# First projection of a decoder layer: waiting for the transposed activations block by block

## The chip, the cores and the metric

The kernel runs on one core of a Trainium2 chip. The metric is device time in microseconds (us), the median of several executions; lower is better.

## The reference

One layer of a decoder over 512 positions of width 2048, in float32:

```
h    = rmsnorm(x, attn_norm)
proj = einsum('bsd,de->bse', h, w_in)        # q, k, v of group A; q, k, v of group B
out_a = dilated_attention(...)               # 16 heads, three dilated windows, ALiBi
out_b = swa_sink_attention(...)              # 16 heads on 2 kv heads, window 128, sinks
x = x + concat(rmsnorm(out_a), rmsnorm(out_b)) @ w_out
x = x + (silu(h2 @ w_gate) * (h2 @ w_up)) @ w_down,   h2 = rmsnorm(x, ffn_norm)
return rmsnorm(x, final_norm)
```

What matters here is the very beginning: loading x, transposing it, and the first two projections (k and v of group B, 128 columns each).

## The kernel before

Each float32 operand of a large product is kept as two halves that TensorE takes, a rounded one (`_hi`) and the remainder (`_lo`), and a product is three matmuls: hi·hi, hi·lo, lo·hi (`three`, lines 285 to 287). ScalarE (ACT) makes the hi half with an activation, VectorE (DVE) the lo half from it.

**Weights** come in units of 512x128, one DMA of 256 KB each, into one of four slots of `raw`. `split` turns a slot into `w_hi` (ACT, L601) and `w_lo` (DVE, L878); a reload of a slot waits for `w_lo`. A unit (u4, slot) serves four blocks of 128 rows of the contraction. Four units make one projection. In what follows unit 0 to 3 is the first projection (bank Q), unit 4 to 7 the second (bank K).

**x** comes in eight DMAs of 512 KB (`x_loaded[0..7]`), each with two blocks k of 128 columns. The SP queue issues ident, then x pieces 0, 1, weight (0,0), x 2, 3, weight (0,1), x 4, 5, weight (0,2), x 6, 7, weight (0,3), then the weights of units 4 to 7. For each block k of the 16, `turn_x` does four TensorE transposes into one of four PSUM banks (L295), `x_high` makes `h_hi` on ACT with the gain of the norm (L606), `x_low` makes `h_lo` on DVE (L882), and signals `xt_lo_done`, which frees the bank for block k+4. The gains themselves arrive as rows, are transposed on TensorE (L488) and copied by DVE (L1062, `gains_done`); every `x_high` needs them.

**Order on TensorE (PE):** blocks 0 to 7 are transposed first (with the gains after block 1). Unit 0 then waits for its four blocks at once, unit 0's twelve matmuls follow, then transposes 8 to 11, unit 1, transposes 12 to 15, unit 2, unit 3. Units 4 to 7 follow, with one thing before unit 7: `spread_r` (L302), eight instructions that spread 1/rms over a bank and wait for `wide_done`. After that the attention pairs begin.

**Order on ACT:** x_high 0-3; w_hi of (0,0) and (0,1); x_high 4-7; w_hi (0,2); four squares of x (L614); x_high 8-11; w_hi (0,3), (1,0); x_high 12-15; w_hi (1,1); four squares; eight small DMA issues; w_hi (1,2); four squares. The last of these squares lets DVE form the row means, GpSimd (POOL) the power, and DVE `widen_r` (L908, `wide_done`).

**Order on DVE:** four memsets, the copy of the gains, x_low 0-3, w_lo (0,0), (0,1), and so on in the order of ACT. Both queues are written out by hand, and every instruction waits its turn.

Of the kernel before, what the change touches and what calls it, by code (L numbers as in the profile page):

```python
# [6 lines left out]
ACT = mybir.ActivationFunctionType  # L7
# [5 lines left out]
P = 128  # L13
# [10 lines left out]
KD = D // P  # L24
# [18 lines left out]
BANK_Q, BANK_K, BANK_V = 0, 1, 4  # L43
# [3 lines left out]
BANK_X = (2, 3, 5, 7)  # L47
BANK_GATE, BANK_UP = (2, 5), (3, 7)

START_SPLITS = ([(0, 0), (0, 1)], [(0, 2)], [(0, 3), (1, 0)], [(1, 1)])  # L50
FIRST_SQ = 4 * (NC - 1)

LAST = [(t, n) for n in range(NC) for t in (0, 1)] + [(t, n) for t in (2, 3) for n in range(NC)]
# [16 lines left out]
def build(nc, x, attn_norm, w_in, sinks, out_norm_a, out_norm_b, w_out, ffn_norm,  # L70
# [4 lines left out]
    def sb(name, shape, dt=F32, at=None):  # L75

        place = spot[0] if at is None else at
        size = int(np.prod(shape[1:])) * BYTES
        t = nc.alloc_sbuf_tensor_at(name, shape, dt, offset=place)
        if at is None:  # L80
            spot[0] = place + (size + 31) // 32 * 32
        assert place + size <= nc.sbuf_usable_end, name
        ends[name] = place + size
        return t

    ends = {}
    ident = sb("ident", [P, P])
    ones = sb("ones", [P, P])
# [5 lines left out]
    tick = sb("tick", [P, 20])  # L94
# [5 lines left out]
    w_hi = sb("w_hi", [P, RING, UNIT], F32R)  # L100
    w_lo = sb("w_lo", [P, RING, UNIT], F32R)
    place_x = spot[0]
    h_hi = sb("h_hi", [P, KD, SEQ], F32R)
    place_y = spot[0]
    h_lo = sb("h_lo", [P, KD, SEQ], F32R)
# [7 lines left out]
    x_first = sb("x_first", [P, NT, D], at=place_o)  # L113
# [41 lines left out]
    bank = [nc.alloc_psum_tensor(f"bank{i}", [P, 512], F32) for i in range(8)]  # L155

    def sem(name):
        return nc.alloc_semaphore(name)

    raw_loaded = [sem(f"raw_loaded{i}") for i in range(RING)]  # L160
    w_hi_done, w_lo_done, w_used = sem("w_hi_done"), sem("w_lo_done"), sem("w_used")
    x_loaded = [sem(f"x_loaded{i}") for i in range(2 * NC)]
    x_again = [sem(f"x_again{i}") for i in range(NC)]
    consts_loaded, ident_loaded, ones_done, gains_loaded = sem("consts_loaded"), sem("ident_loaded"), sem("ones_done"), sem("gains_loaded")
    xt_ready, xt_hi_done, xt_lo_done = sem("xt_ready"), sem("xt_hi_done"), sem("xt_lo_done")
    sq_done, sq_last_done, total_done, mean_done, inv_done = sem("sq_done"), sem("sq_last_done"), sem("total_done"), sem("mean_done"), sem("inv_done")
    wide_done, rbc_ready, rbc_done = sem("wide_done"), sem("rbc_ready"), sem("rbc_done")
    acc_taken, gains_turned, gains_done = sem("acc_taken"), sem("gains_turned"), sem("gains_done")
# [22 lines left out]
    gain_rows = probs[0]  # L191
# [13 lines left out]
    def x_bank(k, base):  # L205

        return bank[(BANK_G if base and k >= KD - 4 else BANK_X)[k % 4]]
# [74 lines left out]
    def _(pe):  # L282
        def three(out_ap, st_hi, st_lo, mv_hi, mv_lo, start, stop):

            nc.tensor.matmul(out_ap, st_hi, mv_hi, start=start, stop=False, skip_group_check=True)  # L285
            nc.tensor.matmul(out_ap, st_hi, mv_lo, start=False, stop=False, skip_group_check=True)  # L286
            return nc.tensor.matmul(out_ap, st_lo, mv_hi, start=False, stop=stop, skip_group_check=True)  # L287

        def turn_x(src, k, base):

            if base + k >= 4:
                pe.wait_ge(xt_lo_done, base + k - 3)
            b = x_bank(k, base)
            for t in range(NT):
                mm = nc.tensor.transpose(b[:, P * t:P * (t + 1)], src[:, t, P * k:P * (k + 1)], ident[:, :])  # L295
            mm.then_inc(xt_ready, 1)

        def spread_r(wide, count, b):

            pe.wait_ge(wide_done, count)  # L300
            for t in range(NT):
                mm = nc.tensor.matmul(bank[b][:, P * t:P * (t + 1)], wide[:, t, :], ident[:, :], start=True, stop=True)  # L302
            mm.then_inc(rbc_ready, 1)

        def tall_unit(u4, j, b, hh, hl):

            pe.wait_ge(w_lo_done, 4 * u4 + j + 1)
            for k in range(4):
                ws = slice(P * k, P * (k + 1))
                mm = three(bank[b][:, :], w_hi[:, j, ws], w_lo[:, j, ws], hh[:, 4 * j + k, :], hl[:, 4 * j + k, :],  # L310
                           j == 0 and k == 0, j == 3 and k == 3)
            mm.then_inc(w_used, 1)
# [143 lines left out]
        def pair(p, a, kv):  # L456

            for c, b in enumerate((BANK_Q, BANK_K, BANK_V, BANK_K)):
# [7 lines left out]
                for j in range(4):  # L466
# [6 lines left out]
                    if a is None and c == 3 and j == 2:  # L473
# [2 lines left out]
                        n = KD + 2 * PAIRS  # L476
                        nc.tensor.transpose(bank[BANK_PT][:, 0:n], gain_rows[0:n, P:2 * P], ident[0:n, 0:n]).then_inc(gains_turned, 1)

        pe.wait_ge(ident_loaded, 16)

        for k in range(8):
            if k % 2 == 0:
                pe.wait_ge(x_loaded[k // 2], 16)
            turn_x(x_first, k, 0)
            if k == 1:

                pe.wait_ge(gains_loaded, 16)
                nc.tensor.transpose(bank[BANK_Q][:, 0:KD], gain_rows[0:KD, 0:P],  # L488
                                    ident[0:KD, 0:KD]).then_inc(gains_turned, 1)
        pe.wait_ge(gains_done, 1)  # L490
        for s in range(8):
            if s < 4:
                pe.wait_ge(xt_lo_done, 4 * s + 4)
            tall_unit(s // 4, s % 4, (BANK_Q, BANK_K)[s // 4], h_hi, h_lo)
            if s < 2:
                for k in range(8 + 4 * s, 12 + 4 * s):
                    if k % 2 == 0:
                        pe.wait_ge(x_loaded[k // 2], 16)
                    turn_x(x_first, k, 0)
            if s == 6:  # L500
                pe.wait_ge(xt_lo_done, KD)
                spread_r(squares[:, :].rearrange("p (t c) -> p t c", c=P), 1, BANK_PT)
# [10 lines left out]
        for g in range(4):  # L513
            for s in range(16):
# [3 lines left out]
                if g == 1 and s == 2:  # L518
# [3 lines left out]
                    for i, kind in enumerate("AB"):  # L522
                        for t in range(NT):
                            mm = nc.tensor.matmul(bank[BANK_PT][:, 4 * i + t:4 * i + t + 1],
                                                  sq_sum[kind][:, P * t:P * (t + 1)], ones[:, 0:1], start=True, stop=True)
# [69 lines left out]
    def _(act):  # L595
        def split(u4, s, wait_slot=True):

            act.wait_ge(raw_loaded[s], 16 * (u4 + 1))
            if wait_slot:
                act.wait_ge(w_used, 4 * u4 + s - 3)  # L600
            nc.scalar.activation(w_hi[:, s, :], raw[:, s, :], ACT.Copy).then_inc(w_hi_done, 1)  # L601

        def x_high(hi, k, base, g0):

            act.wait_ge(xt_ready, base + k + 1)
            nc.scalar.activation(hi[:, k, :], x_bank(k, base)[:, :], ACT.Copy,  # L606
                                 scale=gains[:, g0 + k:g0 + k + 1]).then_inc(xt_hi_done, 1)
# [42 lines left out]
        def pt_high(a, h, r):  # L650
            kind, _, r0 = HEAD[h]
            n = P * sum(len(q) for _, q, _ in (PT_A if kind == "A" else PT_B)[r])
            act.wait_ge(pt_ready, ROUNDS * a + r0 + r + 1)
            if not (isinstance(a, int) and a == 0 and r0 + r < 2):
                act.wait_ge(pv_done, ROUNDS * a + r0 + r - 1)
            nc.scalar.activation(pt_hi[:, (r0 + r) % 2, 0:n], bank[BANK_PT][:, 0:n], ACT.Copy).then_inc(pt_hi_done, 1)  # L656
# [93 lines left out]

        act.dma_start(gain_rows[0:KD, 0:P], attn_norm[0, :].rearrange("(k p) -> k p", p=P)).then_inc(gains_loaded, 16)

        act.wait_ge(gains_done, 1)
        for n in range(NC):
            for k in range(4 * n, 4 * n + 4):
                x_high(h_hi, k, 0, G_ATTN)
            for u4, slot in START_SPLITS[n]:
                split(u4, slot, wait_slot=u4 > 0)
# [115 lines left out]
    def _(dve):  # L874
        def split(u4, s):

            dve.wait_ge(w_hi_done, 4 * u4 + s + 1)
            nc.vector.tensor_tensor(w_lo[:, s, :], raw[:, s, :], w_hi[:, s, :].bitcast(F32), ALU.subtract).then_inc(w_lo_done, 1)  # L878

        def x_low(hi, lo, k, base, g0):  # L880
            dve.wait_ge(xt_hi_done, base + k + 1)
            nc.vector.scalar_tensor_tensor(lo[:, k, :], x_bank(k, base)[:, :], gains[:, g0 + k:g0 + k + 1],  # L882
                                           hi[:, k, :].bitcast(F32), ALU.mult, ALU.subtract).then_inc(xt_lo_done, 1)
# [68 lines left out]
        def pt_low(a, h, r):  # L952
            kind, _, r0 = HEAD[h]
            n = P * sum(len(q) for _, q, _ in (PT_A if kind == "A" else PT_B)[r])
            buf = (r0 + r) % 2
            low_half(pt_lo[:, buf, 0:n], bank[BANK_PT][:, 0:n], pt_hi[:, buf, 0:n], pt_hi_done, ROUNDS * a + r0 + r + 1, pt_lo_done)
# [100 lines left out]
        for kind in "AB":  # L1057
            for h in range(2):
                rest = slice(DH * (1 - h), DH * (2 - h))
                nc.vector.memset(k_lo[kind][h][rest, :].bitcast(F32), 0.0).then_inc(k_rest_zero, 1)  # L1060
        dve.wait_ge(gains_turned, 1)
        nc.vector.tensor_copy(gains[:, 0:KD], bank[BANK_Q][:, 0:KD]).then_inc(gains_done, 1)  # L1062
        dve.wait_ge(gains_done, 1)
        for n in range(NC):
            for k in range(4 * n, 4 * n + 4):
                x_low(h_hi, h_lo, k, 0, G_ATTN)
            for u4, slot in START_SPLITS[n]:
                split(u4, slot)
# [277 lines left out]
```

## Time and profile before

| | |
|---|---|
| median of 3 runs | 2136.72 us (2136.47 to 2137.04) |
| the profiled execution, its own time | 2136.36 us |
| its span | 2134.6 us |
| PE busy | 2115.2 us, 99% |
| DVE busy, ACT busy | 1029.3 us (48%), 743.7 us (35%) |

The span is what the profile covers; 1.76 us of the profiled execution's own time lie around it. PE is busy nearly all of the span, so what matters is where it is not.

### The profile page before, as it was taken

How to read it: one execution, taken by the hardware profiler on the slowest of the kernel's cores; microseconds unless marked ns; L12 is line 12 of the kernel's file. 1: busy time of each engine (PE TensorE's matmuls, PEld its weight loads, DVE VectorE, ACT ScalarE, POOL GpSimd, SP SyncE). 2: the span in 40 equal slices, each digit the busy share in tenths (PEclk: the TensorE clock that was granted, in tenths of full speed). 3: DMA queues.
4: the chain of work that ended last, by engine and by line, in shares of the span. 5: the costliest groups of instructions: out<-in, count | busy, mean ns of one | idle time of the engine just before them, and what ended most of it. 6: DMA issues, size and time to landing. Idle time of an engine off the chain costs nothing.

```text
span 2134.6 us, 29372 instructions
## 1 busy us (share of the span) xinstructions
PE 2115.2 (99%) x9718; PEld 1754.6 (82%) x9718; DVE 1029.3 (48%) x1944; ACT 743.7 (35%) x1436; POOL 117.6 (6%) x191
## 2 busy tenths in 40 slices
PE   8999999999999999999999999999999999999998
PEld 6888888887888888888888888888888888888886
DVE  5466666667765443343433434344343343434436
ACT  5455555554335322222222222222222222222223
POOL 0022222221100000000000000000000000000000
PEclk9999999999999999999999999999999999999999
DMA  6322222224222333333333333323333333332333
GB/s 184 93 74 70 74 74 75 74 73 149 84 94 88 111 99 95 98 98 94 98 96 95 98 95 96 98 94 98 97 95 95 98 97 98 94 98 97 95 99 128
DMA packets 300437, 205.99 MB, mean 97 GB/s; under 512 B 12336, under 2 KB 266592, under 8 KB 299872
## 3 DMA queue, kind: packets, MB, share of 16 engines
q1 hardware_dynamic: 297168, 198.82, 30.8%
q10 hardware_dynamic: 3216, 6.47, 0.8%
q8 instruction: 32, 0.52, 0.1%
q14 instruction: 21, 0.17, 0.0%
HBM read 201.05 MB, written 4.19 MB: 96 GB/s over the span
## 4 chain that ended last, share of the span: by engine, by line
PE 87%; issue 5%; DVE 4%; ACT 3%; DMA 0%; SPq 0%; DVEq 0%; ACTq 0%; POOLq 0%; POOL 0%
PE bank L285 19%; PE bank L287 19%; PE bank L286 19%; PE bank L332 9%; PE bank L334 9%; PE bank L333 9%; PE bank L361 1%; ACT probs L644 1%; ACT w_hi L601 1%; DVE w_lo L878 1%; PE bank L378 1%; PE bank L377 1%; DVE h_lo L882 0%; ACT qB_both L622 0%; DVE pt_lo L887 0%
## 5 line engine op out<-in xcount | busy, mean ns | idle before, releaser
L878 DVE TENSOR_TENSOR w_lo<-raw,w_hi 128x512 fp32r<-128x512 f32 x716 | 496.5, 694 | 1032.5 <-ACT w_hi L601 1031.6
L601 ACT ACTIVATE w_hi<-raw 128x512 fp32r<-128x512 f32 x716 | 451.1, 631 | 1160.0 <-PE bank L287 747.3
L285 PE MATMUL bank<-h_hi,w_hi 128*128 128x512 f32 x1952 | 766.8, 393 | 0.9 <-DVE h_lo L882 0.9
L287 PE MATMUL bank<-h_hi,w_lo 128*128 128x512 f32 x1952 | 760.6, 390 | 0.0
L286 PE MATMUL bank<-h_lo,w_hi 128*128 128x512 f32 x1952 | 760.5, 390 | 0.0
L287 PEld LDWEIGHTS bank<-h_hi,w_lo 128*128 128x128 f32 x1952 | 366.4, 188 | 77.6
L285 PEld LDWEIGHTS bank<-h_hi,w_hi 128*128 128x128 f32 x1952 | 366.6, 188 | 74.9 <-DVE h_lo L882 1.7
L286 PEld LDWEIGHTS bank<-h_lo,w_hi 128*128 128x128 f32 x1952 | 366.8, 188 | 72.9
L332 PE MATMUL bank<-w_hi,act_hi 128*128 128x512 f32 x896 | 350.3, 391 | 1.7 <-DVE y_a L1110 1.3
L334 PE MATMUL bank<-w_hi,act_lo 128*128 128x512 f32 x896 | 348.8, 389 | 0.0
L333 PE MATMUL bank<-w_lo,act_hi 128*128 128x512 f32 x896 | 348.7, 389 | 0.0
L332 PEld LDWEIGHTS bank<-w_hi,act_hi 128*128 128x128 f32 x896 | 168.2, 188 | 37.1 <-issue 2.6
L334 PEld LDWEIGHTS bank<-w_hi,act_lo 128*128 128x128 f32 x896 | 168.2, 188 | 35.4
L333 PEld LDWEIGHTS bank<-w_lo,act_hi 128*128 128x128 f32 x896 | 168.3, 188 | 34.2
L1116 DVE TENSOR_TENSOR x_res<-bank,x_res 128x512 f32<-128x512 f32 x160 | 99.0, 681 | 0.0
L1268 POOL TENSOR_TENSOR inv<-mean,half 128x1 f32<-128x1 f32 (+2 forms) x7 | 5.8, 839 | 1605.4 <-DVE mean L1227 1428.8
L644 ACT ACTIVATE probs<-bank,low 128x256 f32<-128x256 f32 (+3 forms) x128 | 61.1, 486 | 81.1 <-DVE low L936 51.1
L1276 POOL TENSOR_SCALAR probs<-probs,inv_den 128x256 f32<-128x256 f32 (+3 forms) x128 | 81.3, 652 | 0.0
L845 ACT ACTIVATE act_hi<-act_s 128x512 fp32r<-128x512 f32 x43 | 27.2, 632 | 95.5 <-DVE act_s L1172 95.5
L936 DVE CUSTOM_DVE_ANT_0 bank<-bank,bias 128x256 f32<-128x256 f32 (+3 forms) x128 | 53.3, 459 | 0.2
L887 DVE TENSOR_TENSOR pt_lo<-bank,pt_hi 128x512 fp32r<-128x512 f32 (+1 forms) x80 | 48.1, 601 | 3.3 <-ACT pt_hi L656 2.8
L361 PE MATMUL bank<-ident,probs 128*128 128x128 f32 x272 | 43.5, 275 | 1.2 <-DVE pt_lo L887 1.1
(132 smaller groups left out, 1119.8 us busy)
## 6 DMA issues: line engine op xcount, KB each, us to landing
raw<-in_w_gate SPq DMA_DIRECT2D x176, 256.0 KB, 2.9
raw<-in_w_up SPq DMA_DIRECT2D x176, 256.0 KB, 2.9
raw<-in_w_down SPq DMA_DIRECT2D x176, 256.0 KB, 2.4
raw<-in_w_in SPq DMA_DIRECT2D x136, 256.0 KB, 2.9
raw<-in_w_out SPq DMA_DIRECT2D x64, 256.0 KB, 2.5
x_first<-in_x SPq DMA_DIRECT2D x8, 512.0 KB, 7.5
x_res<-in_x ACTq DMA_DIRECT2D x4, 1024.0 KB, 10.9
out_x<-x_res SPq DMA_DIRECT2D x3, 1024.0 KB, 3.9
```

The lines of the kernel that those rows point to most:

```text
L285: nc.tensor.matmul(out_ap, st_hi, mv_hi, start=start, stop=False, skip_group_check=True)
L286: nc.tensor.matmul(out_ap, st_hi, mv_lo, start=False, stop=False, skip_group_check=True)
L287: return nc.tensor.matmul(out_ap, st_lo, mv_hi, start=False, stop=stop, skip_group_check=True)
L332: nc.tensor.matmul(b[:, :], act_hi[:, k, ts], w_hi[:, k, :], start=k == 0, stop=False, skip_group_check=True)
L333: nc.tensor.matmul(b[:, :], act_hi[:, k, ts], w_lo[:, k, :], start=False, stop=False, skip_group_check=True)
L334: mm = nc.tensor.matmul(b[:, :], act_lo[:, k, ts], w_hi[:, k, :], start=False, stop=k == 3, skip_group_check=True)
L361: mm = nc.tensor.transpose(bank[BANK_PT][:, c0 + P * n:c0 + P * (n + 1)], probs[h % 2][:, e:e + P], ident[:, :])
L601: nc.scalar.activation(w_hi[:, s, :], raw[:, s, :], ACT.Copy).then_inc(w_hi_done, 1)
L644: nc.scalar.activation(probs[h % 2][:, e:e + keys], bank[bk][:, c0:c0 + keys], ACT.Exp, bias=low[:, col], scale=-1.0, accum_out=den[:, col ...
L878: nc.vector.tensor_tensor(w_lo[:, s, :], raw[:, s, :], w_hi[:, s, :].bitcast(F32), ALU.subtract).then_inc(w_lo_done, 1)
L1116: nc.vector.tensor_tensor(xt, b, xt, ALU.add).then_inc(grp_taken, 1)
L1276: nc.gpsimd.tensor_scalar(row, row, inv_den[:, 4 * h + b:4 * h + b + 1], 1.0, ALU.mult, ALU.mult).then_inc(p_ready, 1)
```

## The change

It has three parts. (1) On TensorE only blocks 0 to 3 are transposed ahead; unit j then runs block by block, each block's three matmuls waiting for that block's `h_lo`, and after the second and the fourth block of units 0 to 2 the next two blocks are transposed. (2) ACT splits weight unit (0,0) before it waits for the gains, after a one-element activation on `tick` that brings the table load forward. (3) DVE splits (0,0) before it copies the gains.

```diff
-START_SPLITS = ([(0, 0), (0, 1)], [(0, 2)], [(0, 3), (1, 0)], [(1, 1)])
+START_SPLITS = ([(0, 1)], [(0, 2)], [(0, 3), (1, 0)], [(1, 1)])
...
+        def turn_two(k0):
+
+            pe.wait_ge(x_loaded[k0 // 2], 16)
+            for k in (k0, k0 + 1):
+                turn_x(x_first, k, 0)
+
+        def first_unit(j):
+
+            pe.wait_ge(w_lo_done, j + 1)
+            for k in range(4 * j, 4 * j + 4):
+                pe.wait_ge(xt_lo_done, k + 1)
+                ws = slice(P * (k % 4), P * (k % 4 + 1))
+                mm = three(bank[BANK_Q][:, :], w_hi[:, j, ws], w_lo[:, j, ws], h_hi[:, k, :], h_lo[:, k, :], k == 0, k == KD - 1)
+                if j < 3 and k % 2:
+                    turn_two(k + 3)
+            mm.then_inc(w_used, 1)
+
         pe.wait_ge(ident_loaded, 16)
-
-        for k in range(8):
-            if k % 2 == 0:
-                pe.wait_ge(x_loaded[k // 2], 16)
-            turn_x(x_first, k, 0)
-            if k == 1:
-
-                pe.wait_ge(gains_loaded, 16)
-                nc.tensor.transpose(bank[BANK_Q][:, 0:KD], gain_rows[0:KD, 0:P],
-                                    ident[0:KD, 0:KD]).then_inc(gains_turned, 1)
+        turn_two(0)
+        pe.wait_ge(gains_loaded, 16)
+        nc.tensor.transpose(bank[BANK_Q][:, 0:KD], gain_rows[0:KD, 0:P],
+                            ident[0:KD, 0:KD]).then_inc(gains_turned, 1)
+        turn_two(2)
         pe.wait_ge(gains_done, 1)
-        for s in range(8):
-            if s < 4:
-                pe.wait_ge(xt_lo_done, 4 * s + 4)
-            tall_unit(s // 4, s % 4, (BANK_Q, BANK_K)[s // 4], h_hi, h_lo)
-            if s < 2:
-                for k in range(8 + 4 * s, 12 + 4 * s):
-                    if k % 2 == 0:
-                        pe.wait_ge(x_loaded[k // 2], 16)
-                    turn_x(x_first, k, 0)
+        for s in range(4):
+            first_unit(s)
+        for s in range(4, 8):
+            tall_unit(1, s % 4, BANK_K, h_hi, h_lo)
             if s == 6:
...
+        act.wait_ge(ones_done, 1)
+        nc.scalar.activation(tick[:, 18:19], ones[:, 0:1], ACT.Copy)
+        split(0, 0, wait_slot=False)
         act.wait_ge(gains_done, 1)
...
+        split(0, 0)
         dve.wait_ge(gains_turned, 1)
         nc.vector.tensor_copy(gains[:, 0:KD], bank[BANK_Q][:, 0:KD]).then_inc(gains_done, 1)
```

## Rows read from the trace of the kernel before

**Rows 1.** Busy time by stretch: start:end, us, then each engine (xinstructions), granted clock

```profile
0.00:40.00 40.00, 32.48 (x164) 26.19 (x165) 23.91 (x47) 25.15 (x52) 2.38 (x9) 1.00 0.68 201
40.00:2134.60 2094.60, 2082.68 (x9555) 1728.40 (x9554) 1005.35 (x1898) 718.51 (x1384) 115.26 (x182) 1.00 0.31 95
```

**Rows 2.** PE's waits after 40 us, the longest of seven: total, times, longest

```profile
PE bank L332 <- DVE y_a L1110: 1.3, 1, 1.3
```

**Rows 3.** Timeline of PE: start us, us, engine, line, instruction, count

```profile
7.09 1.97 PE L295 MATMUL bank<-ident,x_first 128*128 128x128 f32 x8
9.29 1.11 PE L295 MATMUL bank<-ident,x_first 128*128 128x128 f32 x8 [0.23 <-DMA x_first<-in_x]
...
14.60 1.91 PE L295 MATMUL bank<-ident,x_first 128*128 128x128 f32 x16
16.27 0.48 PE L285 MATMUL bank<-h_hi,w_hi 128*128 128x512 f32 x1
...
20.61 2.54 PE L295 MATMUL bank<-ident,x_first 128*128 128x128 f32 x16 [1.34 <-DVE h_lo L882]
...
26.32 0.50 PE L285 MATMUL bank<-h_hi,w_hi 128*128 128x512 f32 x1 [0.43 <-DVE h_lo L882]
...
29.18 0.39 PE L285 MATMUL bank<-h_hi,w_hi 128*128 128x512 f32 x1
...
37.12 0.39 PE L287 MATMUL bank<-h_hi,w_lo 128*128 128x512 f32 x1
37.47 1.13 PE L302 MATMUL bank<-ident,squares 128*128 128x128 f32 x8
38.35 0.48 PE L285 MATMUL bank<-h_hi,w_hi 128*128 128x512 f32 x1
```

**Rows 4.** Timeline of ACT

```profile
7.47 2.42 ACT L606 ACTIVATE h_hi<-bank,gains 128x512 fp32r<-128x512 f32 x4
...
11.67 0.63 ACT L601 ACTIVATE w_hi<-raw 128x512 fp32r<-128x512 f32 x1 [1.26 <-DMA raw<-in_w_in]
12.21 2.41 ACT L606 ACTIVATE h_hi<-bank,gains 128x512 fp32r<-128x512 f32 x4
15.59 0.63 ACT L601 ACTIVATE w_hi<-raw 128x512 fp32r<-128x512 f32 x1 [0.97 <-DMA raw<-in_w_in]
...
19.00 2.40 ACT L606 ACTIVATE h_hi<-bank,gains 128x512 fp32r<-128x512 f32 x4
...
24.60 0.67 ACT L601 ACTIVATE w_hi<-raw 128x512 fp32r<-128x512 f32 x1
...
31.22 0.63 ACT L601 ACTIVATE w_hi<-raw 128x512 fp32r<-128x512 f32 x1 [3.07 <-issue]
```

**Rows 5.** Timeline of DVE

```profile
7.20 0.17 DVE L1062 COPY gains<-bank 128x16 f32<-128x16 f32 x1 [3.87 <-PE bank L488]
8.28 2.73 DVE L882 SCALAR_TENSOR_TENSOR h_lo<-bank,gains,h_hi 128x512 fp32r<-128x512 f32 x4 [0.90 <-ACT h_hi L606]
...
12.34 0.69 DVE L878 TENSOR_TENSOR w_lo<-raw,w_hi 128x512 fp32r<-128x512 f32 x1 [0.73 <-ACT w_hi L601]
12.95 2.72 DVE L882 SCALAR_TENSOR_TENSOR h_lo<-bank,gains,h_hi 128x512 fp32r<-128x512 f32 x4
...
19.71 2.73 DVE L882 SCALAR_TENSOR_TENSOR h_lo<-bank,gains,h_hi 128x512 fp32r<-128x512 f32 x4 [2.77 <-ACT h_hi L606]
...
23.55 2.72 DVE L882 SCALAR_TENSOR_TENSOR h_lo<-bank,gains,h_hi 128x512 fp32r<-128x512 f32 x4
...
31.96 0.69 DVE L878 TENSOR_TENSOR w_lo<-raw,w_hi 128x512 fp32r<-128x512 f32 x1 [2.28 <-ACT w_hi L601]
...
36.45 0.87 DVE L908 TENSOR_SCALAR squares<-ones,inv 128x128 f32<-128x128 f32 x4 [1.24 <-POOL inv L1268]
```

**Rows 6.** Issue of weight unit (0,0) on the SP queue

```profile
2.19 0.51 SPq L242 DMA_DIRECT2D raw<-in_w_in  x1
```

**Rows 7.** The same issue: KB, us from issue to landing

```profile
raw<-in_w_in SPq DMA_DIRECT2D x1, 256.0 KB, 5.5
```

## Prediction

> **What bounds the kernel now.** I read the busy time by stretch first. After 40 us PE is busy 2082.68 of 2094.60 us; in the first 40 us it is idle 40.00 − 32.48 = 7.52 us [rows 1]. So this is a PE-bound kernel with a slow start, and the change touches only the start. Then the waits of PE after 40 us: the longest is 1.3 us and its releaser is an engine that itself follows PE [rows 2], not a clock time. I take from this that a shift d of the instant at which PE gets going for good arrives at the end as d, neither shrunk nor grown.
>
> That makes one question: at what instant does PE start its last uninterrupted run? The timeline of PE answers it. Units 4, 5 and 6 run from 29.18 to 37.12 + 0.23 = 37.35 us without a hole, then comes `spread_r` at 37.47, then unit 7 at 38.35 [rows 3]. The spread needs `widen_r`, which ran from 36.45 for 0.87 us, to 37.32 [rows 5]. So two things end together: PE's own work (37.35) and the chain of row means (37.32). The reader should see that PE has no lead there. Finishing units 0 to 3 earlier moves only the first of the two.
>
> What feeds the second? Followed back in the timeline of ACT [rows 4]: the last four squares stand right behind w_hi (1,2) at 31.22, that behind eight DMA issues, these behind w_hi (1,1) at 24.60 and four squares, and that behind x_high 8-15 and two w_hi from 19.00, four squares, and w_hi (0,2) at 15.59. The last one that waited for something outside ACT is this one, 0.97 us for its weight to land. From 15.59 us ACT runs one job after another. The whole start hangs on ACT: whatever makes ACT late after 15.59 shifts the spread, and nothing in the change can make the landing at 15.59 earlier, since the DMA order is kept and the only reloads (units 4 up) stand behind it in the SP queue.
>
> **The change part by part.** *ACT and DVE split (0,0) first.* The weight is issued at 2.19 and lands 5.5 us later, at 7.69 [rows 6, 7]. ACT starts it at about 7.72 (0.03 after landing, my allowance). DVE starts w_lo 0.67 us after w_hi starts (11.67 to 12.34 [rows 4, 5]), at 8.39. Behind it on DVE's queue stands the copy of the gains, which ran at 7.20 before [rows 5]. The next DVE instruction after a w_lo starts 0.61 later (12.34 to 12.95 [rows 5]), so the copy is at 9.00, and x_high 0 starts 0.27 after the copy starts (7.20 to 7.47 [rows 4, 5]): 9.27 us in place of 7.47. So the split that was put ahead costs 1.80 us at x_high 0. The table load moves to the first microseconds, where ACT has nothing to do; it was not the last wait before x_high 0 (the copy was), so I cost it at nothing, and what covers it is the wait for the 7.69 landing.
>
> x_high 0-3 take 4 x 0.575 = 2.30 us (7.47 to the w_hi that followed them; the same pace as 19.00 onwards), to 11.57. w_hi (0,1) waits for its landing and starts at 11.67, exactly as before [rows 4]. Up to here nothing is lost on ACT.
>
> *The transposes between the matmuls.* Before, transposes 4-7 were done by 11.9 us, and x_high 4 started at 12.21 right after w_hi (0,1) [rows 4]. Now transposes 4, 5 stand behind blocks 0, 1 of unit 0 on PE, and 6, 7 behind blocks 2, 3. I count the round trip from the start of x_high 0 to the start of x_high 6:
> - x_high 0 to x_low 0: 0.81 (7.47 to 8.28 [rows 4, 5])
> - x_low to the block's first matmul: x_low 15 starts at 23.55 + 3 x 0.66 = 25.53 and its reader at 26.32: 0.79 [rows 3, 5]
> - four blocks of three matmuls, restart after idling included: 26.32 to 29.18 = 2.86 [rows 3]
> - the pair of transposes (4, 5) between them: half of 16.27 − 14.60 = 0.84, and 0.08 for the first matmul behind them (0.48 against 0.39): 0.92 [rows 3]
> - transpose 6, start to complete and seen by ACT: 16 take 1.91 with starts 0.104 apart, so one lasts 0.34, and the fourth ends at 0.65 [rows 3]
>
> Together 6.03: x_high 6 starts at 15.30, x_high 7 0.575 later, and ACT is free for w_hi (0,2) at 9.27 + 6.03 + 1.15 = 16.45. It was 15.59. **First term: +0.86 us.** (x_low's pace of 0.66 is shorter than a block's 0.69, so DVE doesn't add to it.)
>
> *Second round.* ACT's four squares of 3 us cover the same round trip for transposes 8-11: they stand behind unit 1's blocks and end at about 19.6, before ACT wants 9 to 11. But transposes 12-15 stand behind blocks 8-11 of unit 2, and these need x_high 8, which comes only after the squares. Round trip from x_high 8 to x_high 14: 0.71 (19.00 to 19.71 [rows 4, 5]) + 0.79 + 2.86 + 0.92 + 0.65 = 5.93, plus x_high 14 and 15, 1.15: 7.08 us from x_high 8 to w_hi (1,1). Before it was 24.60 − 19.00 = 5.60 [rows 4], with nothing to wait for, as transposes 12-15 then stood ahead of unit 2. **Second term: +1.48 us.**
>
> From w_hi (1,1) on, ACT's list is unchanged: w_hi (1,2) moves from 31.22 to 33.56, w_lo (1,2) from 31.96 to 34.30, `widen_r` from 36.45 to 38.79, the spread from 37.47 to 39.81, unit 7 from 38.35 to 40.69.
>
> *What PE gains on the way.* The reader of x_low 15 was followed by three more blocks; now only its own remains. x_high 14 is at 19.00 + 0.86 + 5.93 = 25.79, x_low 15 at 25.79 + 0.71 + 0.66 = 27.16, its block at 27.95, and unit 4 starts at 28.6 in place of 29.18. So the change does what it says, by 0.6 us. Units 4 and 5 end at 34.1; unit 6 then waits for w_lo (1,2) until about 35.1 and ends at 37.9; PE stands idle until the spread at 39.8. The 0.6 us and more are lost in these two new waits. The rest of what is queued behind them (w_lo (1,3) and the reloads of pair 0) has over 5 us until its reader, so I cost it at nothing.
>
> **The sum:** 0.86 + 1.48 = +2.34 us. On the profiled execution's own time: 2136.36 + 2.34 = 2138.70. The median of the runs stands 0.36 above that execution, so for a median I give 2139.1 us.
>
> *Unknown costs.* The trace of before has no block-wise waits inside a unit. Fourteen of them stand ahead of transposes 14, 15. Below: a gain is excluded, since the same matmuls are only made to wait; nothing is the value I take, as 26.32 to 29.18 shows weight loads running ahead. Above: 0.11 each (the restart in 26.32's 0.50 against 0.39 [rows 3]), on the eight that lie inside the two round trips: +0.9 us.
>
> **PE's clock.** After transposes 0-3 PE now stands idle from 9.06 to about 10.9. In the trace 8 transposes took 1.97 us at 7.09 and 1.11 us at 9.29 [rows 3], that is first the 1.2 GHz level and then the 2.4 GHz one (the granted column reads 1.00 for both [rows 1]). The rise came between 9.06 and 9.29, with only transposes before it, and it held through the pause of 1.34 us ahead of 20.61, behind which 16 transposes with waits among them took 2.54 us. So I cost the new pause, somewhat longer, at nothing. The Trainium skill (TensorE: Matmul & The Clock Gate, Part 4: PE-mode transpose) says that transposes don't count as activity for the gate, so that the full clock doesn't come from them; the pace in the trace speaks against it, as only transposes preceded the rise. By that rule unit 0's first matmuls would run at the low level; it is the last rival below.
>
> **The rivals.**
> - *Only one of the two waits opens.* If x_high 4-7 are in time after all: +1.48, 2138.2; if 12-15 are: +0.86, 2137.6. For it: each rests on margins of about a microsecond. Against: both are chains of dependences with known prices. Chance 0.10.
> - *No change.* Neither opens and ACT keeps its time; unit 4 then starts at 29.18 − 2.1 = 27.1, but the spread still waits for 37.32: at most 0.1 us comes of it. Time 2136.7. It needs both round trips to be shorter by a third. 0.10.
> - *It gains, the other side.* The spread isn't what PE waits for, and the three blocks (3 x 0.69 = 2.06 us) taken from behind x_low 15 reach the end: 2134.7. It decides if ACT stays at 15.59 and `wide_done` comes earlier than 35.3. Against it: the 37.32 and 37.35 that coincide, and ACT without a pause. 0.04. Even this is within 0.2%.
> - *The clock stays low.* If PE works at the low level until transposes 4, 5 are done, two blocks (2 x 0.69) and a pair (0.92) take twice as long: +2.3 on top, 4.6 in all, 2141.4. If all of the first round trip does: 2.86 + 0.92 + 0.65 = 4.4 on top, 2143.5. 0.08.
>
> **How the numbers follow.** My forecast has 0.68. Its own range is +1.3 (each round trip 0.5 shorter) to +3.3 (the unknown waits), 2138.0 to 2140.1. To hold 8 in 10 and the bounds I take in the half case and the no-change case below, and part of the clock case above: 2136.7 to 2140.8. A change of this kernel's time of under 0.2%, 4.3 us, is what I count as the same. The forecast and the first three rivals all lie inside; only the clock case lies above it. Faster 0.01, same 0.90, slower 0.09.
>
> **What would show it.** In the changed kernel's timeline: the copy of the gains at 9.0 and x_high 0 at 9.3; ACT waiting for PE (transposes) ahead of x_high 4, 6 and 14; w_hi (0,2) at 16.4, not 15.6; w_hi (1,1) at 26.9; unit 4 earlier than 29.18; PE idle ahead of unit 6 for `w_lo` and ahead of the spread for `squares` (L302), which starts at 39.8; unit 7 at 40.7. After that, all as before with 2.3 us added. The prediction is wrong if ACT reaches w_hi (0,2) at its landing, if 12-15 are transposed in time, or if the pace of unit 0's first matmuls is that of the low clock.

## The result

The changed kernel took 2140.9 us (median of 15 runs, 2138.4 to 2142.4) against 2136.6 for the kernel before (15 runs, 2136.2 to 2137.8): a ratio of 1.0019, 95% interval 1.0011 to 1.0027. It is slower, by 4.3 us of medians, right at the bound of 0.2% that the prediction counted as the same. The most likely value, 2139.1 us, was too low, and the upper end of the range, 2140.8, stood 0.1 us below the median. The single runs scatter over 4 us.

The profiled execution took 2141.04 us, 4.68 more than the one of before. ACT's timeline in the changed kernel (L608 is w_hi, L613 is x_high):

```profile
1.19 1.28 ACT L761 ACT_TABLE_LOAD   x1 [1.19 <-PEq L1346]
...
8.44 0.63 ACT L608 ACTIVATE w_hi<-raw 128x512 fp32r<-128x512 f32 x1 [5.75 <-DMA raw<-in_w_in]
9.91 2.42 ACT L613 ACTIVATE h_hi<-bank,gains 128x512 fp32r<-128x512 f32 x4 [0.84 <-DVE gains L1073]
...
15.29 1.27 ACT L613 ACTIVATE h_hi<-bank,gains 128x512 fp32r<-128x512 f32 x2 [2.29 <-PE bank L295]
17.57 1.27 ACT L613 ACTIVATE h_hi<-bank,gains 128x512 fp32r<-128x512 f32 x2 [1.01 <-PE bank L295]
18.73 0.63 ACT L608 ACTIVATE w_hi<-raw 128x512 fp32r<-128x512 f32 x1
...
22.14 2.41 ACT L613 ACTIVATE h_hi<-bank,gains 128x512 fp32r<-128x512 f32 x4
...
25.93 1.27 ACT L613 ACTIVATE h_hi<-bank,gains 128x512 fp32r<-128x512 f32 x2 [0.34 <-PE bank L295]
28.09 1.26 ACT L613 ACTIVATE h_hi<-bank,gains 128x512 fp32r<-128x512 f32 x2 [0.90 <-PE bank L295]
29.25 0.63 ACT L608 ACTIVATE w_hi<-raw 128x512 fp32r<-128x512 f32 x1
```

The reader is to see four new waits for PE's transposes (2.29, 1.01, 0.34 and 0.90 us), where between 12.21 and 24.60 the kernel before waited only for the load of (0,2), 0.97 us [rows 4], and where they lead: w_hi (0,2) stands at 18.73 in place of 15.59, w_hi (1,1) at 29.25 in place of 24.60. The same in DVE's timeline (L1073 is the copy of the gains, behind the split; L918 is the widening):

```profile
9.11 0.69 DVE L888 TENSOR_TENSOR w_lo<-raw,w_hi 128x512 fp32r<-128x512 f32 x1 [5.77 <-ACT w_hi L608]
9.71 0.17 DVE L1073 COPY gains<-bank 128x16 f32<-128x16 f32 x1
...
36.56 0.69 DVE L888 TENSOR_TENSOR w_lo<-raw,w_hi 128x512 fp32r<-128x512 f32 x1 [2.93 <-ACT w_hi L608]
...
41.05 0.87 DVE L918 TENSOR_SCALAR squares<-ones,inv 128x128 f32<-128x128 f32 x4 [1.24 <-POOL inv L1279]
```

The copy of the gains moved from 7.20 to 9.71, the widening from 36.45 to 41.05 [rows 5]. And PE:

```profile
7.13 1.70 PE L295 MATMUL bank<-ident,x_first 128*128 128x128 f32 x8
11.62 0.57 PE L285 MATMUL bank<-h_hi,w_hi 128*128 128x512 f32 x1 [2.78 <-DVE h_lo L892]
11.98 0.63 PE L286 MATMUL bank<-h_lo,w_hi 128*128 128x512 f32 x1
12.41 0.63 PE L287 MATMUL bank<-h_hi,w_lo 128*128 128x512 f32 x1
...
15.79 0.40 PE L286 MATMUL bank<-h_lo,w_hi 128*128 128x512 f32 x1
16.02 0.39 PE L287 MATMUL bank<-h_hi,w_lo 128*128 128x512 f32 x1
...
37.31 0.50 PE L285 MATMUL bank<-h_hi,w_hi 128*128 128x512 f32 x1 [0.54 <-DVE w_lo L888]
...
42.07 1.13 PE L302 MATMUL bank<-ident,squares 128*128 128x128 f32 x8 [1.73 <-DVE squares L918]
```

Both foretold waits are there: 0.54 us for w_lo ahead of unit 6, 1.73 us for the row means ahead of the spread, which starts at 42.07 in place of 37.47 [rows 3]. That is 4.60 of the 4.68 us; after it the difference stays. What wasn't in the sum stands in the second to fourth line: behind PE's pause of 2.78 us the first matmuls start 0.43 us apart and last 0.63, later 0.23 and 0.39. The busy time by stretch has the same in its clock column (third from the right):

```profile
11.84:15.25 3.41, 3.41 (x12) 2.71 (x12) 2.20 (x4) 1.13 (x2) 0.00 (x0) 0.50 1.12 334
15.25:17.00 1.75, 1.75 (x11) 1.45 (x10) 0.99 (x2) 1.27 (x2) 0.00 (x0) 1.00 1.10 345
```

A granted clock of 0.50 is the 1.2 GHz level, 1.00 is 2.4 GHz. In this execution the clock had risen while transposes 0 to 3 ran (the eight at 7.13 take 1.70 us, where the kernel before took 1.97 [rows 3]; the trace records the rise at 8.43), and behind the pause it was down again, from 11.84 to 15.25. The 4.65 us at w_hi (1,1) split so, each part a difference of two starts: x_high 0 at 9.91, where the walk had 9.27: 0.64, nearly all of it the load of (0,0), which landed 6.2 us after its issue and not 5.5; from x_high 0 to x_high 6 (17.57) 7.66 in place of the walk's 6.03: 1.63, the low clock; the walk's own first term, 0.86; and from x_high 8 to w_hi (1,1) 7.11 against 5.60 before: 1.51, the second term, foretold as 1.48.

### The profile page after: what moved, and what is told of

Its sections match the earlier page's. It is cut to its first block, busy times and chain, and to the rows that moved or that the text cites. A ratio compares the mean times of both kernels' runs of the same rounds, so it can differ in the third digit from the quotient of the medians.

```text
span 2139.2 us, 29373 instructions
## 1 busy us (share of the span) xinstructions
PE 2115.9 (99%) x9718; PEld 1755.6 (82%) x9718; DVE 1029.5 (48%) x1944; ACT 744.4 (35%) x1437; POOL 117.9 (6%) x191
## 4 chain that ended last, share of the span: by engine, by line
PE 87%; issue 5%; DVE 4%; ACT 4%; ACTq 0%; DMA 0%; DVEq 0%; POOL 0%; SPq 0%; POOLq 0%
PE bank L285 19%; PE bank L287 19%; PE bank L286 19%; PE bank L332 9%; PE bank L333 9%; PE bank L334 9%; ACT w_hi L608 1%; ACT probs L651 1%; PE bank L361 1%; DVE w_lo L888 1%; PE bank L378 1%; PE bank L377 1%; ACT qB_both L629 0%; DVE pt_lo L897 0%; ACT probs L621 0%
## 5 line engine op out<-in xcount | busy, mean ns | idle before, releaser
L608 ACT ACTIVATE w_hi<-raw 128x512 fp32r<-128x512 f32 x716 | 450.9, 631 | 1163.3 <-PE bank L287 747.2
L334 PEld LDWEIGHTS bank<-w_hi,act_lo 128*128 128x128 f32 x896 | 168.2, 188 | 35.2
```

What stands on the lines that cost most here:

```text
L334: mm = nc.tensor.matmul(b[:, :], act_lo[:, k, ts], w_hi[:, k, :], start=False, stop=k == 3, skip_group_check=True)
```

## The experiments

Each kernel ran beside the kernel before on the same chip; the kernel before had medians of 2136.7, 2136.9 and 2137.3 us in the three groups (31 to 33 runs each). The 95% interval of a ratio stands in brackets behind it. Below, "against before" is the difference of medians within a group; for the changed kernel it was 4.3, and 3.6 in the last group.

**A filled pause.** The changed kernel, with work for PE where it stood idle:

```diff
         turn_two(2)
+        for _ in range(12):
+            nc.tensor.transpose(bank[6][:, 0:P], ident[:, :], ident[:, :])
         pe.wait_ge(gains_done, 1)
```

> The changed kernel with 12 extra transposes of ident into an unused PSUM bank, put where PE stands idle ahead of unit 0. If PE's pause from 8.8 to 11.6 us lets its clock fall to the 1.2 GHz level, the fill keeps it at 2.4: unit 0's first matmuls start 0.23 us apart (0.43 in the changed kernel), x_high 6 starts 6.0 us after x_high 0 (7.7 there), the median falls from 2140.9 by about 1.6 to 2139.3 us and the scatter of 4 us goes with it. If transposes do not count as activity, or the scatter comes from when the loads land, the pace stays at 0.43 or the scatter stays, near 2140.9.

Measured: 2138.94 us (2138.55 to 2140.28, 11 runs), ratio 1.0011 (1.0001 to 1.0020), 2.2 against before. PE, then ACT (L610 is w_hi, L615 is x_high):

```profile
9.00 1.88 PE L503 MATMUL bank<-ident 128*128 128x128 f32 x12
10.82 0.47 PE L285 MATMUL bank<-h_hi,w_hi 128*128 128x512 f32 x1
11.13 0.40 PE L286 MATMUL bank<-h_lo,w_hi 128*128 128x512 f32 x1
11.36 0.40 PE L287 MATMUL bank<-h_hi,w_lo 128*128 128x512 f32 x1
...
39.70 1.13 PE L302 MATMUL bank<-ident,squares 128*128 128x128 f32 x8 [1.74 <-DVE squares L920]
```

```profile
7.65 0.63 ACT L610 ACTIVATE w_hi<-raw 128x512 fp32r<-128x512 f32 x1 [4.95 <-DMA raw<-in_w_in]
9.12 2.42 ACT L615 ACTIVATE h_hi<-bank,gains 128x512 fp32r<-128x512 f32 x4 [0.84 <-DVE gains L1075]
...
15.19 1.27 ACT L615 ACTIVATE h_hi<-bank,gains 128x512 fp32r<-128x512 f32 x2 [0.91 <-PE bank L295]
16.34 0.63 ACT L610 ACTIVATE w_hi<-raw 128x512 fp32r<-128x512 f32 x1
...
26.88 0.63 ACT L610 ACTIVATE w_hi<-raw 128x512 fp32r<-128x512 f32 x1
```

The pace is 0.23 us from the first matmuls on. The fill did not keep the clock up, it brought it up: its transposes start 0.21 us apart up to 9.64 and 0.11 apart from 9.84 on, and the trace records the rise at 9.81. x_high 6 comes 6.07 us after x_high 0, and the scatter is 1.7 us in place of 4. This execution, with an early load and full-pace matmuls, is the one the prediction walked through: w_hi (0,2) at 16.34 (16.45 foretold), w_hi (1,1) at 26.88 (26.88), the spread at 39.70 (39.81), and the whole took 2138.66 us (2138.70). So the walk was right for a PE at full clock and an early load; a low clock in unit 0 is what it lacked. Unit 4 starts here at 28.75, earlier than before's 29.18, as foretold; in the changed kernel's own trace, with the low clock, it starts at 31.13, later than before.

**The splits of (0,0) back in their old place.** The block-wise part of the change alone:

```diff
-START_SPLITS = ([(0, 1)], [(0, 2)], [(0, 3), (1, 0)], [(1, 1)])
+START_SPLITS = ([(0, 0), (0, 1)], [(0, 2)], [(0, 3), (1, 0)], [(1, 1)])
...
-        nc.scalar.activation(tick[:, 18:19], ones[:, 0:1], ACT.Copy)
-        split(0, 0, wait_slot=False)
...
-        split(0, 0)
         dve.wait_ge(gains_turned, 1)
```

> The block-wise matmuls and interleaved transposes alone: the split of (0,0) is back behind x_high 0-3 on ACT and x_low 0-3 on DVE. My theory (ACT waits for transposes that stand behind matmuls): x_high 0 is back at 7.5, but unit 0 can't start before w_lo (0,0) at 11.7, so transpose 6 comes no earlier: +1.7 in the first round trip, +1.5 in the second, with the clock's fall about +1.6 more: 2139.8 to 2141.4 us, as slow as the changed kernel. Rival (the split put ahead of the gains is what costs): its 1.8 us come back and only the second term stays, 2138.1 us.

Measured: 2142.28 us (2141.29 to 2142.79, 9 runs), ratio 1.0025 (1.0015 to 1.0035), 5.6 against before, and above the expected 2139.8 to 2141.4. The rival, 2138.1, is refuted. ACT and PE in its trace:

```profile
7.80 2.42 ACT L613 ACTIVATE h_hi<-bank,gains 128x512 fp32r<-128x512 f32 x4
...
15.63 1.27 ACT L613 ACTIVATE h_hi<-bank,gains 128x512 fp32r<-128x512 f32 x2 [1.46 <-PE bank L295]
```

```profile
12.03 0.77 PE L285 MATMUL bank<-h_hi,w_hi 128*128 128x512 f32 x1 [2.64 <-DVE w_lo L885]
```

x_high 0 is back at 7.80, but transposes 4 to 7 stand behind unit 0, and unit 0 now waits for w_lo (0,0). So the interleaving makes ACT late without the early split too, and the early split didn't cause the loss: with it the median is 1.2 to 1.9 us lower, counted against before.

**Transposes 12 to 15 ahead of unit 2**, as before, all else as changed:

```diff
-                if j < 3 and k % 2:
+                if j < 2 and k % 2 and k + 3 < 12:
                     turn_two(k + 3)
...
         for s in range(4):
+            if s == 2:
+                turn_two(12)
+                turn_two(14)
             first_unit(s)
```

> The changed kernel with transposes 12 to 15 ahead of unit 2, as they stood in the kernel before; all else as changed. My theory: the second term goes, ACT doesn't wait ahead of x_high 12 and 14, w_hi (1,1) comes 5.6 us after x_high 8 (7.1 in the changed kernel), the time is 1.5 below the changed kernel's, 2139.4 us. Rival (PE's own work sets the end, ACT is no matter): unit 2 starts later by the transposes, the time stays at 2140.9 or grows.

Measured: 2140.08 us (2137.22 to 2142.34, 11 runs), ratio 1.0012 (1.0003 to 1.0021), 3.4 against before. ACT (L616 is x_high, L611 is w_hi):

```profile
22.63 2.40 ACT L616 ACTIVATE h_hi<-bank,gains 128x512 fp32r<-128x512 f32 x4
...
25.95 2.43 ACT L616 ACTIVATE h_hi<-bank,gains 128x512 fp32r<-128x512 f32 x4
28.22 0.67 ACT L611 ACTIVATE w_hi<-raw 128x512 fp32r<-128x512 f32 x1
```

From x_high 8 to w_hi (1,1) it is 5.59 us again, with no wait: the second term is gone, as expected. The median, with 5 us of scatter around it, shows 0.3 to 1.0 of the 1.5 us. In this execution the clock stayed low until 16.96, and x_high 6 came 8.94 us after x_high 0 in place of 7.66; the run with both repairs, below, shows the term better.

**The block waits alone**, in the kernel before (transposes and splits in the old order; `first_unit` as in the change, without `turn_two`):

```diff
...
-            if s < 4:
-                pe.wait_ge(xt_lo_done, 4 * s + 4)
-            tall_unit(s // 4, s % 4, (BANK_Q, BANK_K)[s // 4], h_hi, h_lo)
+            if s < 4:
+                first_unit(s)
+            else:
+                tall_unit(1, s % 4, BANK_K, h_hi, h_lo)
```

> The kernel before with only the waits of units 0 to 3 made block by block; order of transposes and splits as before. My theory: unit 4 starts 0.8 to 0.9 us earlier (28.3 in place of 29.18), PE then waits for the row means ahead of the spread, which stays at 37.5: no change, 2136.6 us within 0.2. Rival (the spread isn't the gate): 2135.7 us.

Measured: 2137.7 us (2136.27 to 2138.15, 11 runs), ratio 1.0003 (0.9994 to 1.0012): no change that can be told, though the median came out 1.0 above before, where 0.2 was allowed. The rival, a gain to 2135.7, is refuted. PE in its trace:

```profile
36.55 0.39 PE L287 MATMUL bank<-h_hi,w_lo 128*128 128x512 f32 x1
37.65 1.13 PE L302 MATMUL bank<-ident,squares 128*128 128x128 f32 x8 [0.71 <-DVE squares L918]
```

Unit 4 starts at 28.62 and unit 6 ends at 36.78 in place of 37.35, and PE stands idle for 0.71 us until the row means are there. What the block waits save is given back at the spread.

**The row means earlier**, alone and with the block waits. Eight DMA issues on ACT go behind the last four squares:

```diff
-        for dst, src in ((dist, c_dist), (lnm, c_lnm), (band, c_band), (slope, c_slope), (sink, sinks[0, :].partition_broadcast(P))):
-            act.dma_start(dst[:, :], src).then_inc(consts_loaded, 16)
-        for src, r0, n in ((ffn_norm, 0, KD), (out_norm_a, KD, PAIRS), (out_norm_b, KD + PAIRS, PAIRS)):
-            act.dma_start(gain_rows[r0:r0 + n, P:2 * P], src[0, :].rearrange("(k p) -> k p", p=P)).then_inc(gains_loaded, 16)
         for s in range(3, 8):
             split(*ahead(s // 4, s % 4))
             if s == 3:
                 x_square(x_first, 2, probs[1][:, 0:512], 0)
+                for dst, src in ((dist, c_dist), (lnm, c_lnm), (band, c_band), (slope, c_slope), (sink, sinks[0, :].partition_broadcast(P))):
+                    act.dma_start(dst[:, :], src).then_inc(consts_loaded, 16)
+                for src, r0, n in ((ffn_norm, 0, KD), (out_norm_a, KD, PAIRS), (out_norm_b, KD + PAIRS, PAIRS)):
+                    act.dma_start(gain_rows[r0:r0 + n, P:2 * P], src[0, :].rearrange("(k p) -> k p", p=P)).then_inc(gains_loaded, 16)
```

> The kernel before with the eight small DMA issues on ACT (3.07 us of its time) moved behind the last four squares, nothing else. The row means come 3 us earlier, widen_r ends at 34.3, but PE is busy with unit 6 until 37.35: the spread moves from 37.47 to about 37.4, the time by at most 0.1: 2136.6 us. If PE waited for the means in the kernel before by more than it seems, up to 3 us are gained.

> The same with the block-wise waits of units 0 to 3 as well (transposes and splits in the old order). Each edit alone changed nothing or should change nothing; if my reading is right that PE's work and the row means end together in the kernel before, both at once give what the block waits save on PE, 0.8 to 0.9 us: unit 4 at 28.3, spread at 36.6, 2135.8 us. Rival (the block waits save nothing real): 2136.6 us.

Measured: 2136.8 us (2136.1 to 2137.8, 11 runs), ratio 0.9999 (0.9989 to 1.0008), for the issues alone; 2136.25 us (2135.19 to 2136.8, 11 runs), ratio 0.9996 (0.9987 to 1.0005), for both. The medians are 0.1 and 0.7 below before. Neither interval excludes no change, but the order is the expected one, and the fastest run with both, 2135.19, lies below all 33 of before (2136.24 at the least). In the trace with both, the row means are there at 35.2 and the spread waits for nothing:

```profile
34.36 0.87 DVE L918 TENSOR_SCALAR squares<-ones,inv 128x128 f32<-128x128 f32 x4 [1.24 <-POOL inv L1278]
```

```profile
13.85 0.63 PE L286 MATMUL bank<-h_lo,w_hi 128*128 128x512 f32 x1
14.27 0.63 PE L287 MATMUL bank<-h_hi,w_lo 128*128 128x512 f32 x1
...
37.69 1.05 PE L302 MATMUL bank<-ident,squares 128*128 128x128 f32 x8
```

The foretold 36.6 for the spread is not seen here, since in this execution x landed late and unit 0, from 13.27, ran at half pace too, although transposes 4 to 7 stand ahead of it as before.

**The same move of the DMA issues in the changed kernel.**

> The changed kernel with the eight DMA issues behind the last squares. My theory: PE's two new waits (0.5 us ahead of unit 6, 1.7 ahead of the spread) go, the spread starts when unit 6 ends, 8.2 us after unit 4; 2.5 to 2.8 us of the changed kernel's loss come back: 2138.3 us. Rival (the loss sits in the units' own waits and the low clock alone): it stays at 2140.9 us.

Measured: 2139.81 us (2137.26 to 2141.71, 11 runs), ratio 1.0013 (1.0004 to 1.0022), 2.9 against before. PE:

```profile
39.97 1.05 PE L302 MATMUL bank<-ident,squares 128*128 128x128 f32 x8
41.53 0.50 PE L285 MATMUL bank<-h_hi,w_hi 128*128 128x512 f32 x1 [0.51 <-DVE w_lo L888]
```

From w_hi (1,1), at 29.91 here, the spread comes 10.06 us later and not 12.82: the wait for the row means is gone, and the way to the spread is 2.8 us shorter, as expected. But 0.51 us of wait turn up again ahead of unit 7, since w_hi (1,3) now stands behind the eight issues, and the median gained about 1, not 2.5. The theory that PE waits for the row means holds; my price for moving the issues left out what they are moved past. That is a part of what is missing; this execution also reached w_hi (1,1) 0.66 us later than the changed kernel's, with the clock low until 16.63, and how the rest of the median's shortfall divides isn't shown.

**The copy of the gains first on DVE**, its split of (0,0) behind it:

```diff
-        split(0, 0)
         dve.wait_ge(gains_turned, 1)
         nc.vector.tensor_copy(gains[:, 0:KD], bank[BANK_Q][:, 0:KD]).then_inc(gains_done, 1)
+        split(0, 0)
```

> The changed kernel with DVE's copy of the gains ahead of its split of (0,0), as it stood before; ACT still splits (0,0) first. x_high 0 then waits only for w_hi (0,0), 8.3 in place of 9.1 to 9.9, so unit 0 starts at about 9.9, PE's pause shrinks from 2.8 to under 1 us, the clock stays at the 2.4 GHz level and ACT is ready for w_hi (0,2) at about its landing: the first term is 0, the second stays 1.5: 2138.1 us. Rival (the pause is no cause of the clock's fall, or the first term comes from elsewhere): 2139.4 to 2140.9 us.

Measured: 2139.87 us (2138.98 to 2142.1, 11 runs), ratio 1.0013 (1.0004 to 1.0022), 2.9 against before. My expectation, 2138.1, failed, and the time lies where its rival had it. ACT and PE:

```profile
9.34 0.63 ACT L608 ACTIVATE w_hi<-raw 128x512 fp32r<-128x512 f32 x1 [6.65 <-DMA raw<-in_w_in]
9.88 2.40 ACT L613 ACTIVATE h_hi<-bank,gains 128x512 fp32r<-128x512 f32 x4
```

```profile
11.56 0.77 PE L285 MATMUL bank<-h_hi,w_hi 128*128 128x512 f32 x1 [2.31 <-DVE h_lo L892]
```

In this execution the load of (0,0) landed at 9.3, so x_high 0 was no earlier than with the copy behind the split, PE paused for 2.31 us, and the matmuls ran at half pace. The rival's reason is not thereby shown: the edit did not shorten the pause as it was to. Even the fastest run, 2138.98, is above 2138.1. What a pause of under 1 us would do in this order was not seen; that part stays open.

**Both repairs at once**: the filled pause and transposes 12 to 15 ahead of unit 2.

> The changed kernel with both repairs: 12 filling transposes ahead of unit 0, transposes 12 to 15 ahead of unit 2. If the loss is the sum of its parts, only the first term at full clock is left, 0.9 us, and the row means come at 38.2: 2137.4 to 2137.6 us, with a scatter under 2 us. If the terms overlap, it stays near the better of the two alone, 2138.9.

Measured: 2137.69 us (2137.06 to 2139.12, 11 runs), ratio 1.0003 (0.9994 to 1.0012), 0.4 against before. The parts add up: 2138.94 with the fill, 1.3 less with the second term gone too (1.8, counted against before), where 1.5 was foretold. The first term alone was to leave 0.9 us; the median shows 0.4. The profiled execution was the slowest, 2139.12, and shows what is left in it:

```profile
9.53 0.63 ACT L613 ACTIVATE w_hi<-raw 128x512 fp32r<-128x512 f32 x1 [6.83 <-DMA raw<-in_w_in]
11.00 2.43 ACT L618 ACTIVATE h_hi<-bank,gains 128x512 fp32r<-128x512 f32 x4 [0.84 <-DVE gains L1078]
```

A load that lands at 9.5 and not 7.65 puts x_high 0 at 11.0. Since the change, ACT's whole order hangs on this landing; before it, (0,0) was wanted only at 9.8, and the landings that ACT waited for were those of (0,1) and (0,2) [rows 4].

**The changed kernel once more.**

> The changed kernel once more, for its scatter and a second profile: 2140.9 us, single runs from 2138.4 (clock at its 2.4 GHz level and loads early) to 2142.4. If the profile shows a low clock after PE's pause again, the time is 2140 or more; if the clock stays high, 2138.4 to 2139.5.

Measured: 2140.89 us (2138.62 to 2142.11, 11 runs), ratio 1.0018 (1.0009 to 1.0027). The profiled execution, 2140.22 us, had the load at 7.9 and still the slow matmuls, and here the clock had not risen before the pause: the eight transposes ahead of it take the 1.97 us of the low level.

```profile
7.08 1.97 PE L295 MATMUL bank<-ident,x_first 128*128 128x128 f32 x8
11.07 0.77 PE L285 MATMUL bank<-h_hi,w_hi 128*128 128x512 f32 x1 [2.02 <-DVE h_lo L892]
11.64 0.63 PE L286 MATMUL bank<-h_lo,w_hi 128*128 128x512 f32 x1
12.06 0.63 PE L287 MATMUL bank<-h_hi,w_lo 128*128 128x512 f32 x1
...
13.77 1.20 PE L295 MATMUL bank<-ident,x_first 128*128 128x128 f32 x8
```

The clock rises while transposes 4 and 5 run (1.20 us for the eight at 13.77; the trace records the rise at 14.11).

**A reordered start, from the kernel before.** The experiments say that ACT's order is what to shorten. ACT does x_high 0-3, w_hi (0,0), (0,1), x_high 4-7, w_hi (0,2) and x_high 8-11 as before, and then what the diff shows. Here x_high 8 no longer waits behind four squares, and the DMA issues stand behind w_hi (1,3); DVE follows. One kernel has the block waits too, the other the old waits.

```diff
...
+        x_square(x_first, 0, probs[1][:, 0:512], 0, range(0, 2))
+        x_high(h_hi, 12, 0, G_ATTN)
+        x_high(h_hi, 13, 0, G_ATTN)
+        split(0, 3, wait_slot=False)
+        x_high(h_hi, 14, 0, G_ATTN)
+        x_high(h_hi, 15, 0, G_ATTN)
+        split(1, 0)
+        x_square(x_first, 0, probs[1][:, 0:512], 0, range(2, 4))
+        split(1, 1)
...
+        x_square(x_first, 1, probs[1][:, 0:512], 0)
...
```

> From the kernel before: block-wise waits, transposes and splits of (0,0) in the old order; on ACT the first four squares leave the place ahead of x_high 8 (two go behind x_high 11, two behind w_hi (1,0)), w_hi (0,3) goes between x_high 13 and 14, and the eight DMA issues stand behind w_hi (1,3); DVE follows that order. By my reading PE then starts transposes 12 to 15 right behind unit 1 (19.1 in place of 20.6) and never waits again: unit 4 at about 26.4, the spread at 34.6, unit 7 at 35.4 in place of 38.35: 2133.7 us. If the row means or w_lo (1,2) are late after all, less: 2135 to 2136 us.

> The same reordering with the old waits, four blocks at a time. x_low 15 ends at 23.5, just when unit 2 does, so the block waits should have nothing left to give: 2133.8 us, as the run with them. If they still give something, it is up to 0.7 us more.

Measured: with block waits 2135.45 us (2133.91 to 2138.28, 11 runs), ratio 0.9994 (0.9985 to 1.0003); with the old waits 2134.73 us (2133.88 to 2136.57, 11 runs), ratio 0.9988 (0.9979 to 0.9997). The second is faster than the kernel before, by 2.6 us of medians (the interval begins at 0.03%), and beats the changed kernel by 6.2 us in the same group. Both medians lie above the 2133.7 and 2133.8 that were foretold; the fastest runs, 2133.91 and 2133.88, reach them. The two don't differ beyond their scatter, so no gain of the block waits can be told there, as expected. In the trace of the first, which is its fastest run, PE does not stop for the row means, and the spread is at 34.42 in place of 37.47 [rows 3]:

```profile
34.42 1.05 PE L302 MATMUL bank<-ident,squares 128*128 128x128 f32 x8
```

## Why the prediction was right and where it was wrong

- *What gates PE.* Right. PE's work and the row means ended together in the kernel before. The block waits alone left 0.71 us of idling ahead of the spread and moved no time; with the means earlier the median fell by 0.7 us, which its interval doesn't tell from nothing.
- *The split put ahead of the gains.* The chain of it was right: copy 0.60 behind w_lo (0.61 foretold), x_high 0 0.20 behind the copy (0.27 foretold). Its start was taken from one landing, 7.69; the executions show (0,0) taken up at 7.65 to 9.53. This step needed a range and had none: in the changed kernel's trace it cost 0.64 on top, the second term of the sum that was off.
- *First term, +0.86.* Right at full clock, 16.34 − 15.59 = 0.75 in the run with the filled pause. In the changed kernel's own trace it measured 3.14: 0.86, 0.64 for the landing, 1.63 for the clock and a rounding.
- *Second term, +1.48.* Right: 1.51 in the changed kernel's trace, and undone by putting transposes 12 to 15 ahead.
- *PE's clock, "I cost the new pause at nothing".* This is the step that failed. Its reason was that the clock had risen with transposes alone and then held through the 1.34 us ahead of 20.61. In the kernel before, the trace records the rise at 9.33, just after transposes 4 and 5 had begun at 9.29 [rows 3], and the change moves these behind unit 0's matmuls. So in five of the six profiled executions with the interleaved order and no fill the clock had not risen when PE's pause began (table at the end), and in the sixth it had, at 8.43, and was down again at 11.84. In all six the first matmuls ran at half pace. The rival that priced it, 2.3 us for two blocks and a pair of transposes, named the right place; it measured 1.63 (x_high 0 to x_high 6 against the walk's 6.03), and 1.42, 2.47 and 2.91 in the second profile, with the DMA issues moved and with transposes 12 to 15 ahead. It had a chance of 0.08, and it was the usual case.
- *The Trainium skill's rule.* The Trainium skill (TensorE: Matmul & The Clock Gate, Part 4: PE-mode transpose) has transposes not count as activity. Its consequence, slow first matmuls, came true in the changed kernel; its reason did not: with nothing but transposes from 5.2 to 10.8 us, the run with the filled pause has the rise at 9.81 and full-pace matmuls at once.
- *The rest at nothing.* Right: the table load, moved to 1.19, covered; the reloads covered; behind the spread the difference stayed, 4.60 us there and 4.68 at the end.
- *What PE gains on the way.* Right at full clock: with the filled pause unit 4 starts at 28.75, foretold 28.6, before 29.18, and PE then waits 0.57 us for w_lo ahead of unit 6 and 1.74 us ahead of the spread. In the changed kernel's own two traces it starts at 31.13 and 30.38: the low clock took more than the block waits gave.
- *The rivals.* No change and a gain are refuted, and so is only one of the two waits: both opened in every trace of a kernel that had both. The clock's rival happened, on top of the forecast, as it was written to, and at less than its price in the changed kernel's own traces.
- *A count.* The prediction has fourteen block-wise waits ahead of transposes 14 and 15; the kernel has twelve. No term used it.
- *The size.* 2.34 was foretold; 4.3 was measured in medians and 4.68 between the profiled executions. Of the 2.34 missing in the latter 1.6 is the clock and 0.6 the landing. Their shares in the median are not settled, as only profiled executions show them; filling the pause took 1.4 to 2.1 us off the median, counted against the kernel before. The median came out 0.1 us from the range's upper end although the sum leaves the clock out: the room above came from "part of the clock case" and from unknown waits that did not show, and in part that is luck.

## What to carry to other kernels

Before making a bound engine wait in finer steps, follow what it will wait for next: here the row means ended with its work, and nothing that it saved could get past them. A producer put behind its consumer's work on the same queue makes a round trip, and each engine on that round trip gets late; count it start to start, and it comes out to 0.1 us. And when an edit takes work away from TensorE shortly after its first instruction, look whether the clock had risen by then in the kernel before, and by which work; if it was the work that is moved, price the matmuls behind the gap at half pace as the likely case, not as a tail.

## What the runs showed that I had not expected

- Mostly the clock did not fall in the pause; it had not risen yet. The trace records when it changes, and the spacing of the transposes (0.21 us at the low level, 0.11 at the full one) agrees. Times in us:

| execution | clock before the pause | pause ahead of unit 0 | unit 0 starts | clock low until |
|---|---|---|---|---|
| changed kernel, first | rises at 8.43, falls at 11.84 | 2.78 | 11.62 | 15.25 |
| changed kernel, second | low | 2.02 | 11.07 | 14.11 |
| splits of (0,0) back | low | 2.64 | 12.03 | 15.10 |
| transposes 12 to 15 ahead | low | 1.52 | 10.83 | 16.96 |
| DMA issues moved | low | 2.09 | 11.43 | 16.63 |
| gains first | low | 2.31 | 11.56 | 17.00 |
| filled pause | rises at 9.81, in the fill | none | 10.82 | |
| both repairs | rises at 10.06, in the fill | 1.78 | 12.70 | |

- The low clock is not only the interleaved order's. Where x lands late, PE pauses among transposes 4 to 7 in the old order too: with the DMA issues moved it waited 1.25 us, and the clock rose at 13.43; in the reordered kernel with the old waits 0.95 us and 14.01; with the issues moved and the block waits 1.35 and 0.42 us, and a clock that had risen at 8.72 was down from 12.14 to 15.55. In the kernel before and two others (rises at 9.33, 9.36 and 8.38) unit 0 ran at full pace. Why the risen clock held through the 1.78 us in the table, and not here or in its first row, the runs don't tell.
- The clock column doesn't always show it. The trace records no level before the first rise, and there the column reads 1.00: over the slow matmuls of the second profile, where the clock had not risen yet, as over the first transposes. It reads 0.50 only where the clock had risen and fell back. The distance of starts is the safer sign:

```profile
11.07:13.77 2.70, 2.70 (x6) 2.02 (x7) 2.43 (x4) 1.36 (x3) 0.00 (x0) 1.00 1.11 343
```

- Loads issued at the same time in the same order land at different times. The load of (0,0), issued at 2.2 us, took 5.5 us in the kernel before [rows 7], 6.2 in the changed one and 7.3 in the run with both repairs. A late landing moves the profiled execution, but it isn't shown to be the main cause of the changed kernel's scatter of 4 us: with the pause filled, on the same path, the scatter is 1.7 and 2.1 us.
